# The copy of the expert values moves from ScalarE's queue to SyncE's, and the expert blocks, rows and value slots are put in another order

## What is computed

```python
proj = einsum('bld,de->ble', xn, w_in)
qkv_a, gate_a, b_a, a_a, q_b, k_b, v_b, gate_b, sel_a, sel_b = split_cols(proj, IN_SIZES)
qkv_a, conv_new = causal_conv(qkv_a, conv_buf, conv_w)          # width 4, SiLU
...                                                             # gated_delta: inverse of I + L per chunk
# PEER, per block of 128 tokens: 8 heads, top 16 of 128 x 128 experts
q = einsum('td,de->te', xb, w_q).reshape(128, 8, 2, 128)
s = einsum('thpd,hpkd->thpk', q, keys)
...                                                             # top 16 of each half, top 16 of the 256 sums
act = gelu(einsum('td,thkd->thk', xb, u_tab[eidx]))
coef = softmax(best) * act
return einsum('thk,thkd->td', coef, v_tab[eidx])
```

## Time and profile before

| | |
|---|---|
| median of 3 runs | 2278.29 us (2277.26 to 2285.83) |
| the profiled execution, its own time | 2285.4 us |
| its span, first to last instruction | 2283.6 us |
| TensorE busy / weight loads | 1960.3 us (86%) / 1591.0 us (70%) |
| VectorE, GpSimd, ScalarE busy | 1397.7, 845.6, 611.5 us |
| mean granted clock of TensorE | 0.941 |
| moved by DMA | 629.24 MB, of which ScalarE's queue (q10) 67.11 MB |

### The profile page before, as it was taken

How to read it: one execution, slowest core, us unless ns; L and a number is a source line. 1 busy time by engine, 2 the same in 40 slices (tenths; PEclk the granted TensorE clock), 3 DMA queues, 4 the chain that set the end, 5 groups by cost and what they waited for, 6 DMA issues and landing times.

```text
span 2283.6 us, 29645 instructions
## 1 busy us (share of the span) xinstructions
PE 1960.3 (86%) x10912; PEld 1591.0 (70%) x10912; DVE 1397.7 (61%) x2791; ACT 611.5 (27%) x1217; POOL 845.6 (37%) x625
## 2 busy tenths in 40 slices
PE   5985586676799878899999999999779998999886
PEld 4985586676699578899999999998724433434332
DVE  3134144221533645358898998989967777777663
ACT  4221231111422442344444444444420000000000
POOL 0001011011000000045465565565547777776563
PEclk9997788887799989999999999999999999999999
DMA  3316415988350154269999999999989999999997
GB/s 116 116 50 212 166 43 184 309 263 297 117 195 24 60 189 144 86 244 347 372 339 356 382 354 359 376 362 347 336 317 411 411 402 409 403 406 412 411 409 287
DMA packets 243881, 629.24 MB, mean 276 GB/s; under 512 B 18946, under 2 KB 136773, under 8 KB 225944
## 3 DMA queue, kind: packets, MB, share of 16 engines
q0 software_dynamic: 74880, 377.52, 42.0%
q1 hardware_dynamic: 152224, 182.80, 23.4%
q10 hardware_dynamic: 16640, 67.11, 8.6%
HBM read 584.36 MB, written 110.21 MB: 304 GB/s over the span
## 4 chain that ended last, share of the span: by engine, by line
PE 24%; DMA 14%; DVE 11%; issue 5%; POOL 2%; ACT 1%; SPq 0%; DVEq 0%; another core or an unknown queue 0%; ACTq 0%; POOLq 0%
DMA ex_uv_row<-value_rows,ex_eidx 11%; PE ps L2129 9%; PE ps L580 5%; PE ps L582 5%; PE ps L581 5%; DVE ex_fin L2379 4%; DMA ex_w_raw<-in_peer_ut 3%; POOL ex_uv_row L2051 2%; DVE ex_uv_row L2367 2%; DVE ex_w_lo L1929 1%; ACT ex_w_hi L2189 0%; DVE ex_q_s L2392 0%; DMA ex_w_raw<-in_peer_wq 0%; DVE ex_hot L2349 0%; DVE ex_top_i L2326 0%
## 5 line engine op out<-in xcount | busy, mean ns | idle before, releaser
L2129 PE MATMUL ps<-ex_uv_row,ex_q_s 128*128 128x512 f32 (+1 forms) x1208 | 544.5, 600 | 76.2 <-DVE ex_q_s L2392 46.3
L2129 PEld LDWEIGHTS ps<-ex_uv_row,ex_q_s 128*128 128x128 f32 (+1 forms) x1208 | 216.9, 187 | 387.7 <-issue 357.1
L2051 POOL DMA_INDIRECT ex_uv_row<-value_rows,ex_eidx x384 | 401.2, 1045 | 195.3 <-issue 95.1
L580 PE MATMUL ps<-x_hi,ex_w_lo 128*128 128x384 f32 (+2 forms) x1296 | 428.0, 330 | 21.1 <-DVE ex_w_lo L1929 15.2
L582 PE MATMUL ps<-x_hi,ex_w_hi 128*128 128x384 f32 (+2 forms) x1296 | 425.0, 328 | 0.0
L581 PE MATMUL ps<-x_lo,ex_w_hi 128*128 128x384 f32 (+2 forms) x1296 | 424.6, 328 | 0.0
L2379 DVE SCALAR_TENSOR_TENSOR ex_fin<-ex_uv_row,ret_tables,ex_fin 128x1024 f32<-128x1024 f32 x218 | 364.2, 1671 | 15.0 <-ACT ret_tables L2219 14.9
L1929 POOL TENSOR_TENSOR ex_w_lo<-ex_w_raw,ex_w_hi 128x1024 fp32r<-128x1024 f32 x72 | 187.9, 2610 | 407.8 <-ACT ex_w_hi L2189 407.2
L580 PEld LDWEIGHTS ps<-x_hi,ex_w_lo 128*128 128x128 f32 x1296 | 245.5, 189 | 26.3 <-DVE ex_w_lo L1929 19.2
L581 PEld LDWEIGHTS ps<-x_lo,ex_w_hi 128*128 128x128 f32 x1296 | 245.8, 190 | 0.0
L582 PEld LDWEIGHTS ps<-x_hi,ex_w_hi 128*128 128x128 f32 x1296 | 245.6, 190 | 0.0
(11 more groups left out here) (415 smaller groups left out, 3630.6 us busy)
## 6 DMA issues: line engine op xcount, KB each, us to landing
value_rows<-in_peer_uv ACTq DMA_DIRECT2D x16, 4096.0 KB
ex_w_raw<-in_peer_ut SPq DMA_DIRECT2D x128, 512.0 KB
value_rows<-ex_z_rows SPq DMA_DIRECT2D x128, 128.0 KB
first_raw<-in_w_in SPq DMA_DIRECT2D x8, 1024.0 KB, 7.8
ex_w_raw<-in_peer_wq SPq DMA_DIRECT2D x16, 512.0 KB
value_rows<-ex_z_rows SPq DMA_DIRECT2D x128, 64.0 KB
dp_w_raw<-in_w_in SPq DMA_DIRECT2D x14, 512.0 KB
ex_uv_row<-value_rows,ex_eidx POOLq DMA_INDIRECT x384
```

The source lines that it names most:

```text
L580: pe.matmul(out, left(llo, c), right(rhi, c), start=(c == 0), stop=False)
L2051: pool.indirect_dma_start(value_slot(p)[0], None, k.value_rows, bass.IndirectOffsetOnAxis(ap=eidx[:, u, n % TOPK:n % TOPK + 1], axis=0), e ...
L2129: ins = pe.matmul(k.pv[j % 2][0:r, c, :], spread[:, on_tensor[p] % SPREADS, 0:r], v[:, c * 512:(c + 1) * 512], start=first, stop=last)
```

## The change

- `copy_values` now issues pieces of 1 MiB (256 rows), 64 of them, on SyncE's queue: one behind each weight chunk in proj_a (8), proj_b (8), branches (8) and w_out (4), one for each side tile of convolve (8), two for each of the solve (28). ScalarE issues none.
- `expert_blocks`: in each of seven groups of 16 blocks two are q blocks, at places 0 and 3; the last 30 blocks are all z.
- A row of pairs goes with every block from the ninth on (`ROWS_FROM` = 8), so all 136 rows go with blocks. The additions of the sample's rows on TensorE come one block later. `unit_schedule` counts blocks instead of z blocks, and the retrieval behind the blocks moves among them.
- `by_dve`: VectorE forms the lower half of two blocks in three (95), GpSimd of one in three (49).
- The value slots: 10 instead of 11, beginning behind the last row's slot of the ring; each of the first gathers waits only for the rows of pairs in whose memory it writes.
- x_rep, the sample's inputs spread over the partitions, gets memory of its own and is loaded at block 12 instead of at the end.

```diff
-VALUES = RING * 2 * D // VALUE_SLOT
+VALUES = 10
+ROWS_FROM = 8
-COPIES = 16
+COPIES = 64
+COPY = NE // COPIES
+COPY_FROM = {"proj_a": 0, "cv": 8, "dp": 16, "proj_b": 44, "branches": 52, "w_out": 60}
+COPIES_BESIDE = {"cv": 1, "dp": 2}
...
-    def copy_values(self, act):
-
-        n = self.copies
-        part = slice(n * NE // COPIES, (n + 1) * NE // COPIES)
-        act.dma_start(self.value_rows[part, P:P + D], self.peer_uv[part, D:2 * D]).then_inc(self.values_copied, 16)
+    def copy_values(self, sp, n):
+
+        part = ds(n * COPY, COPY)
+        sp.dma_start(self.value_rows[part, P:P + D], self.peer_uv[part, D:2 * D]).then_inc(self.values_copied, 16)
...
                                 if n not in late:
                                     sp.dma_start(dst, src).then_inc(done, 16)
+                            k.copy_values(sp, COPY_FROM[name])
+                        k.copy_values(sp, COPY_FROM[name] + chunk0 + 2 * i + b)
...
             self.load(sp, n + 2)
+            for piece in range(self.copies * n, self.copies * (n + 1)):
+                self.k.copy_values(sp, self.copy_from + piece)
             sp.wait_ge(self.taken, 2 * n + 2)
...
-    for u in range(PH):
-        for j in range(TOPK):
-            if u + 1 < PH and j in (0, 2):
-                out.append(("q", 2 * (u + 1) + j // 2))
-            out.append(("z", u * TOPK + j))
-    return out
+    for u in range(PH - 1):
+        out += [("q", 2 * (u + 1) + j // 3) if j in (0, 3) else ("z", next(z)) for j in range(TOPK)]
+    return out + [("z", n) for n in z]
...
-            return i < 2 or (i % 2 == 1 and i >= 5)
+            return i < 2 or (i >= 5 and i % 3 != 0)
...
                     if p >= PAIRS + VALUES:
                         row_used(pool, p - VALUES)
-                    b = (p - PAIRS) % VALUES
+                    else:
+                        slots = range(value_at(b) // (2 * D), (value_at(b) + VALUE_SLOT - 1) // (2 * D) + 1)
+                        for before in range(PAIRS - RING, PAIRS):
+                            if before % RING in slots:
+                                row_used(pool, before)
...
                 pool.wait_ge(k.values_copied, 16 * COPIES)
-                pool.wait_ge(vector_done, HK)
-                pool.wait_ge(v_done, PER_ROW)
...
+                for i in range(len(blocks)):
+                    p = i - ROWS_FROM
+                    if 0 <= p < PAIRS:
+                        dot(p)
                     if 5 <= i + 2 < len(blocks) and by_dve(i + 2):
                         lower(dve, i + 2)
+                    if 0 < p <= HK:
                         add_vector(p - 1)
```

More of the change, by code:

```diff
@@ L2277, in _ @@
                         upper(i + 2)
[L2278 to L2281 removed]
+                    if 0 <= i - ROWS_FROM < PAIRS:
+                        row(i - ROWS_FROM)
+                    if i in weight_at:
+                        weight(weight_at[i])
                 activate(NE // P - 1)
[L2283 removed]
+                for p in range(len(blocks) - ROWS_FROM, PAIRS):
                     row(p)
[L2285 removed]
                 root(0)
```

93 lines of the change are left out of this document (38 added, 55 removed).

## The result

| | before | changed |
|---|---|---|
| median, us | 2277.78 (2275.29 to 2285.83) | 2159.36 (2157.10 to 2165.02) |
| ratio, 95% interval | | 0.9478 (0.9447 to 0.9509) |
| profiled execution, its span | 2285.4, 2283.6 | 2161.43, 2159.6 |
| mean granted clock | 0.941 | 0.966 |

The account below looks back on a forecast made before the run. Limits differed: TensorE in w_in stages and blocks of U, waits for side weights in convolution and half the solve, bandwidth in V's gathers. Terms -52 -64 -6 +7 +4 -15 = -126 us gave 2152 us, range 2112 to 2207.

Parts of the forecast that it names:

- Convolution -52: Convolution: four slow tiles of 20.1 us become fast ones of 7.1 us, saving 52 us.
- Solve -64: Solve: 0.87 of the 73.1 us of waits for side weights is on the path, saving 64 us.
- I stay at the good end: Convolution and solve: tiles are slower than the transfers, so loads do not wait out the copy, 105 us in all otherwise.
- Rival d: Convolution and solve: each side load waits for the copy ahead of it, +105 us, 2257 us; chance 0.06.
- e: Every stage: weights come behind the copy, all 64 pieces exposed, about 2398 us, slower than before; chance 0.04.
- f: Convolution and solve: the waits for side weights stay though the pieces are small, 2274 us; chance 0.03.
- proj_b +7: Start of proj_b: two copy pieces of 3.5 us stand uncovered ahead of first_raw's second chunk, costing 7 us.
- Blocks and seam -15: Blocks of U and the gap before V's gathers: -24 seam, +12 sample rows on TensorE, -3 stalls, together -15 us.
- Rival b: Blocks of U bound by DMA: +24 us, 2176 us, chance 0.12; sign: last block over 15 us later after the first.
- 1.5 us each. 23 fewer: -35 us: Blocks, VectorE: each GpSimd subtraction lengthens VectorE's work by 1.5 us, so 23 fewer save it 35 us.
- Rival c: Gathers of V: paced by slots, so ten for eleven cost 58 us, 2210 us; chance 0.05.
- Rival a: Convolution and solve: shorter waits keep TensorE's clock up, a further -25 us, 2127 us; chance 0.15.

Follow-up runs that it names:

- copy_second_job: Changed kernel, but in proj_b and branches no copy pieces behind the first job's chunks, two behind each chunk of the second: 2145.47 us, ratio 0.94.
- lower_late: Changed kernel, but VectorE forms its lower half behind the addition, as before the change: 2167.34 us, ratio 0.9541.
- slots8: Changed kernel with 8 value slots instead of 10: 2160.53 us, ratio 0.9505.
- pool_lower_first: Changed kernel, but GpSimd forms its lower half ahead of the block's gather of a row of pairs, not behind it: 2183.7 us, ratio 0.9611.

## Why the prediction was right, point by point

- **Convolution -52: -55.5.** Four slow tiles became fast ones. The tiles come 0.3 us faster than the 7.1 us taken.
- **Solve -64: -66.9.** The fraction of 0.87 was read from one period and was a little low: 66.9 of the 73.1 us of waits are 0.92. End of the solve -6: -4.7, the result still waits 4.3 us to land.
- **"I stay at the good end":** right; a load never waited for the whole of the copy ahead. Rival d is out (landings of 6.2 us at most in convolve), and e with it; so is f (10.7 us of waits are left).
- **proj_b +7: +10.1. branches +4: +4.8.** The mechanism is as put, and copy_second_job takes both away. In proj_b the price of the transfers was right, ScalarE's wait grew by 7.4 us; what the term left out is the clock of 0.50 behind TensorE's wait of 8.2 us, another 2.6 us.
- **Blocks and seam -15: -8.8 in the trace, 2 to 10 us by the medians.** The seam went as worked out (-24: -25.7) and the sample's rows on TensorE too (+12: +10.9). The term that failed is the last one, "TensorE's stalls, some 40 us in the stage, I leave at the same size but for 3 us": its idle time grew by 5.1 us. (Nor was it 40: it was 25.3 us in the stage before.) The waits are for lower halves of both engines and for ScalarE, and ScalarE's waits for weight blocks rose from 91.6 to 150.1 us. Rival b, a stage bound by DMA, did not come with its time: it gave +9 us for blocks and seam, and they are 8.8 us shorter. But the sign named for it came, a last block more than 15 us later after the first than before (16.9), of which the sample's rows are 10.9. And the transfers are near their limit in the middle of the blocks: from 1146 to 1396 us the DMA share is 0.99 to 1.02, where the kernel before has 0.93 to 1.00 from 1207 to 1457. Whether the 5 us are the transfers' stays open.
- **"1.5 us each. 23 fewer: -35 us":** right for the old order (-31 us from before to lower_late), but the change also moves the lower halves, and that the sum did not price. The excess fell by 57 us and the mean addition to 1.31 us, not 1.75. It did no harm because VectorE was not the bound.
- **Gathers of V 0: +0.2.** Rival c is out by the earlier trace rows against 1554.9 to 2135.8 us after, and by slots8.
- **Rival a, the clock:** it did rise, 0.74 to 0.92 in convolve and 0.84 to 1.00 in the solve, but what came beyond my terms is 3.5 + 2.9 + 2.2 = 9 us, not 25. The stretch from 226 to 303 us, where TensorE waits mostly for VectorE, only goes from 0.81 to 0.86. In the waits TensorE had little work that the lower clock could stretch; the step's gain of the clock is already in the step's time of 5.56 us, which I had taken from a free step.

The sum on record was -126, the trace gives -124. That they lie so close is luck in part: the stages before proj_b were 7.3 us better than forecast, the later ones and the blocks 9 us worse. The medians give -118.4. Most of the 7 us between forecast and result is none of the terms: the profiled execution of the kernel before lay 7.1 us above its median, that of the changed kernel 2.1, and a drop read between the two profiles was taken off the median.

## What to carry to other kernels

A weight load that is needed soon should be the one ahead on its queue, and bulk traffic go behind it in small pieces on the same queue: small pieces on another queue or large ones on this one each gave away part of the gain. Beside another queue's transfers, compare packets and not bytes. Put bulk transfers where loads have slack and keep them away from the start of a stage, where loads are late already. An instruction that is moved forward on its engine takes its wait along: price what is queued behind it, as pool_lower_first shows.

## What the hardware did that I had not expected

- A load of 0.5 MiB in 512-byte packets beside 4 MiB in 4096-byte packets of another queue took 18.3 us, nearly the copy's whole length; alone 3.6. In 2 us of it the engines took 145 packets of the one and 141 of the other.
- Behind the 7.5 MiB that SyncE issues at the start of proj_b (the last load of them 4 MiB), the next issue holds it for some 15 us whatever it is: 14.10 us for a load of 1 MiB before, 15.26 for a piece of the copy in the change, 15.33 for the load in copy_second_job. Everything in its program behind waits too. That the queue is full then is my reading; no run varies its fill.
- A wait of TensorE of 8.2 us was followed by a clock of 0.50, which cost 2.6 us more.
- A VectorE instruction with two tensor inputs beside a GpSimd subtraction took up to 3.43 us instead of 1.28. GpSimd's own mean stayed at 2.60 to 2.66 us in all five kernels of the table, whichever instruction of VectorE stood beside it.
